# Thirty-six unread bf16 products behind the pairs of heads of an SSD stage: left out

## The chip, the cores and the metric

The kernel runs on one core of one Trainium2 chip. The metric is the device time of one execution in microseconds (us); the time of the kernel before is the median of its runs. Five engines work beside each other and each takes its own instructions in order: TensorE (PE in the profile, its weight loads PEld) for matrix products, VectorE (DVE), ScalarE (ACT), GpSimd (POOL), and SyncE (SP), which here issues DMA transfers. They wait for each other by semaphores.

## The reference, cut to what matters

Two transformer blocks on 512 latent tokens of width 1024. The first block mixes tokens with two groups of heads: a Mamba-2 (SSD) scan of 16 heads and a gated delta rule (GDN) scan of 8 heads, both forwards and backwards over 256 context and 512 latent tokens; its gated and normalised result goes through an output projection and an MLP. The second block has attention and two smaller mixers. For this change only the SSD scan's output on the latent tokens matters, in chunks of 128 tokens:

```python
seg = acum[:, :, :, None, :] - acum[:, :, None, :, :]
lmat = jnp.exp(jnp.where(causal[:, :, None], seg, -jnp.inf))
scores = jnp.einsum('bcihn,bcjhn->bcijh', C_c, B_c) * lmat
y = (jnp.einsum('bcijh,bcjhp->bcihp', scores, xdt)
     + jnp.einsum('bcihn,bchpn->bcihp', C_c, h_prev) * jnp.exp(acum)[..., None])
```

Per head and chunk: a matrix of decays, times the scores, times the inputs; and the carried state, read by decayed queries.

## The kernel before, in words

The program is one launch with a block of code for each engine; the order on each engine is the order in which its code is written, and nothing reorders it. A projection stage streams weights for the first 496 us, then comes the SSD stage that the change touches (496 to 588 us), then the GDN scan (to 722 us), and then projections and MLPs for the rest.

In the SSD stage four chunks of latent tokens (`ci`, 0 to 3) run one after the other, and in each eight pairs of heads (`b` on PE, `hp` on ACT and DVE). One pair on PE is, in its order:

- `decays` (L1251, L1252) for the pair two places on, two products of 512 columns that make the exponents of the decay matrices of both heads and directions in one PSUM bank. It waits until ACT has read that bank's previous contents.
- L1280, four products that put the skip term of the pair into the output bank; L1285, four products with the decay matrix `wmat` of this pair, which wait until DVE has finished that matrix; L1292, eight products with the carried states.
- until now, L1300: two products whose result goes into columns 128 to 511 of bank 1 and is never read. Nothing waits for them and they wait for nothing. They stand behind the pairs `b` 0 to 6 of chunks 0 and 1 and behind pairs 0 to 3 of chunk 2: 18 pairs, 36 products.

Before pair 7 of chunks 0 and 1, PE also makes the scores of the next chunk (`chunk_scores`, L1234) and the decays of its queries (`state_decays`, L1243); the second half of these follows in pair 0 of the chunk.

ACT takes the exponential of each pair's decays (L1944, into two alternating buffers `lbuf`). DVE adds the two directions (L2598) and multiplies by the scores (L2601), which makes `wmat`. Between two pairs DVE also does other work in its own order: the decayed queries (`cpm`, L2583) at the turn of a chunk, the gating of a finished half chunk (`yfm`, L2570), and, from pair 2 of chunk 0 to pair 1 of chunk 2, two elimination steps a pair of a triangular inverse that the GDN stage needs (L2476, L2480), which end with a copy (L2485, `XT`).

That inverse is stored to memory by SP in four transfers (L828 to L832). At pair 4 of chunk 2 PE runs `corner5` (L1167) for the GDN stage; ACT takes its result over (L1896, `PM`) once `corner5` is done and those four stores have landed. ACT's next work for the SSD pairs stands behind that.

Of the kernel before, what the change touches and what calls it, by code (L numbers as in the profile page):

```python
# [18 lines left out]
P = 128  # L19
# [225 lines left out]
def build_kernel(nc, a, out):  # L245
    ctx = ExitStack()
    with ctx:
# [14 lines left out]
        bank = [ctx.enter_context(nc.psum_tensor(f"bank{i}", [P, 512], F32)) for i in range(8)]  # L262
# [15 lines left out]
        def const(n):  # L278
            i = CF.index(n)
            return cf[:, i * P:(i + 1) * P]  # L280

        def cbf(i, n=1):
            return cb[:, i * P:(i + n) * P]
# [158 lines left out]
        def state_at(slot):  # L442

            return v3(hole[slot // 4], KB)[:, 2 * (slot % 4):2 * (slot % 4) + 2, 0:CTX]
# [209 lines left out]
        def ffn_jobs(l):  # L654
            return [(JOB[f"gu{l}{j}"], JOB[f"dn{l}{j}"]) for j in range(3)]

        width = [kc for _, kc, n, _ in JOBS for _ in range(n)]

        def next_width(u):
# [278 lines left out]
        def _(pe):  # L938
# [72 lines left out]
            def gate_transposes(xs, bk):  # L1011

                for n, x in enumerate(xs):
                    mm = pe.transpose(bk[:, n * P:(n + 1) * P], gparts[:, x * P:(x + 1) * P].bitcast(F32), const("ident"))
                mm.then_inc(gates_full, 1)
# [191 lines left out]
            def first_inverse(ci, b):  # L1207

                if (ci, b) == (2, 4):
                    pe.wait_ge(sc_copied, 3)  # L1210
                    pe.wait_ge(row_parts, 11)
                part = {(2, 4): corner5, (2, 6): block5, (3, 3): corner6, (3, 5): block6_t}.get((ci, b))
                if part is corner6:
                    pe.wait_ge(sc_copied, 4)
                if part is not None:
                    for p in range(2):
                        part(0, p)
# [6 lines left out]
            def chunk_scores(ci):  # L1224

                c = NCTX + ci
                if ci:
                    pe.wait_ge(sc_copied, ci)
                if ci == 2:
                    pe.wait_ge(row_parts, 11)  # L1230
                if ci == 3:
                    pe.wait_ge(dt64_ready, 4)
                for gr in range(2):
                    mm = pe.matmul(bank[gr][:, 0:P], bf[64 * gr:64 * gr + 64, c * P:(c + 1) * P],  # L1234
                                   cfm[64 * gr:64 * gr + 64, ci * P:(ci + 1) * P], start=True, stop=True)
                mm.then_inc(sc_full, 1)

            def state_decays(ci, q):

                for d in range(2):  # L1240
                    need(cp_ready, 1, lag=2)
                    i = ci % 2 * 4 + 2 * d + q
                    pe.matmul(bank[2 + d][:, :], halfsel[i // 4][:, i % 4 * P:(i % 4 + 1) * P], grow[4 + ci // 2][:, :], start=True, stop=True  # L1243
                              ).then_inc(cp_full, 1)

            def decays(n):

                ci, hp = n // KB, n % KB
                need(l_ready, 1, lag=2)
                bk = bank[4 + hp % 2]  # L1250
                pe.matmul(bk[:, :], cbf(0), b4(cbf(1, 2), 2), start=True, stop=False)  # L1251
                pe.matmul(bk[:, :], rowcol(ci % 2 * 8 + hp), grow[2 + ci // 2][:, :], start=False, stop=True).then_inc(l_full, 1)  # L1252

            for ci in range(4):
                c = NCTX + ci
                if ci == 0:
                    pe.wait_ge(eps_lo_ready, 1)
                    decays(0)
                    decays(1)
                    chunk_scores(0)  # L1260
                    pe.wait_ge(row_parts, 9)
                    state_decays(0, 0)
                if ci == 3:
                    chunk_scores(3)
                    state_decays(3, 0)

                for b in range(KB):
                    if b == 7 and ci < 2:
                        chunk_scores(ci + 1)
                        state_decays(ci + 1, 0)  # L1270
                    if KB * ci + b + 2 < 4 * KB:
                        decays(KB * ci + b + 2)
                    gr = b // 4
                    if ci and b % 4 == 0:
                        pe.wait_ge(y_taken, 2 * ci - 1 + gr)
                    heads = [(2 * b + e, bank[6 + gr][64 * e:64 * e + 64, (b % 4) * P:(b % 4 + 1) * P]) for e in range(2)]
                    if b % 4 == 0:
                        pe.wait_ge(xd_ready, 2 * ci + gr + 1)
                    for h, dst in heads:
                        pe.matmul(dst, xd[gr][:, h % 8 * 64:(h % 8 + 1) * 64], const("ident"), start=True, stop=False)  # L1280
                    if b == 0:
                        state_decays(ci, 1)
                    need(w_ready)
                    for h, dst in heads:
                        wm = pe.matmul(dst, xtm[:, c * D + h * 64:c * D + (h + 1) * 64], wmat[h % 8 // 4][:, h % 4 * P:(h % 4 + 1) * P], start=False, stop=False)  # L1285
                    wm.then_inc(w_used, 1)
                    if b in (0, 2):
                        pe.wait_ge(cp_ready, 4 * ci + b + 2)
                    for d in range(2):
                        slot = ci if d == 0 else 3 - ci  # L1290
                        for h, dst in heads:
                            mm = pe.matmul(dst, state_at(d * 4 + slot)[64 * gr:64 * gr + 64, h % 8 // 4, h % 4 * 64:(h % 4 + 1) * 64],  # L1292
                                           cpm[d][h % 8 // 4][64 * gr:64 * gr + 64, h % 4 * P:(h % 4 + 1) * P],
                                           start=False, stop=(d == 1))
                    if b % 4 == 3:
                        mm.then_inc(y_full, 1)
                    first_inverse(ci, b)
                    if (ci, b) < (2, 4) and b < 7:
                        for _ in range(2):
                            pe.matmul(bank[1][:, P:4 * P], cbf(0), cbf(0, 3), start=True, stop=True)  # L1300
                    if (ci, b) == (1, 1):
                        gate_transposes((6, 0), bank[0][:, P:3 * P])

# [210 lines left out]
            for l in range(2):  # L1514
# [43 lines left out]
                for b in range(2):  # L1558
                    for e in range(2):
                        for c in range(4):  # L1560
# [3 lines left out]
                                           start=True, stop=True)  # L1564
# [1516 lines left out]
```

## Time and profile before

| | us |
|---|---|
| median of 3 runs | 2356.0 (2354.25 to 2356.33) |
| profiled execution, its own time | 2358.29 |
| its span, first to last instruction | 2356.5 |
| PE busy in the span | 2274.5 (97%) |
| DVE busy in the span | 1322.6 (56%) |
| ACT busy in the span | 951.6 (40%) |
| mean granted TensorE clock | 0.988 of full speed |

PE is busy nearly throughout because most of the program is weight streaming. The shares are means over stages with different limits, so the SSD stage has to be read by itself, from 499 to 557 us of the span. Two levels of the TensorE clock occur in the records: 1.00 (2.4 GHz) and 0.50 (1.2 GHz).

### The profile page before, as it was taken

What the parts mean: (1) busy time and instruction counts of PE and PEld (TensorE: products, weight loads), DVE (VectorE), ACT (ScalarE), POOL (GpSimd) and SP (SyncE); (2) the same over time, 40 slices, a digit from 0 to 9 for tenths busy, and PEclk for the clock granted to TensorE, in tenths of its full rate; (3) what the DMA queues carried; (4) which work ended last, traced back from release to release, by engine and by line L of the source; (5) the groups of instructions that cost most, each with busy time, mean ns of one, the idle gap of its engine ahead of it and who ended that gap; (6) DMA issues with size and microseconds to landing.
All of it is one profiled execution on the core that took longest, in us unless ns stands there. A gap on an engine that the chain in (4) does not pass through costs nothing.

```text
span 2356.5 us, 31246 instructions
## 1 busy us (share of the span) xinstructions
PE 2274.5 (97%) x12510; PEld 1826.9 (78%) x12510; DVE 1322.6 (56%) x2068; ACT 951.6 (40%) x1625; POOL 166.5 (7%) x150
## 2 busy tenths in 40 slices
PE   5999999988999999999999999999999999999998
PEld 4888886755887878888877578888888658888886
DVE  7677777786677355443456644444454654434445
ACT  3555555456326242332445533222244554222222
POOL 0000000000100100000223020000011302000001
PEclk8999999999999999999999999999999999999999
DMA  6343425532544222223222022223323102222222
GB/s 268 108 134 134 175 85 191 176 110 78 157 139 177 98 86 95 99 98 98 98 97 63 28 72 98 92 97 99 98 93 101 56 19 90 99 99 93 95 98 90
DMA packets 117249, 252.29 MB, mean 107 GB/s; under 512 B 45104, under 2 KB 49968, under 8 KB 116208
## 3 DMA queue, kind: packets, MB, share of 16 engines
q1 hardware_dynamic: 102816, 215.15, 27.6%
q0 software_dynamic: 5136, 18.88, 2.4%
q10 hardware_dynamic: 9152, 16.26, 2.0%
q8 instruction: 100, 1.64, 0.3%
q14 instruction: 45, 0.37, 0.0%
HBM read 225.07 MB, written 25.17 MB: 106 GB/s over the span
## 4 chain that ended last, share of the span: by engine, by line
PE 87%; DVE 6%; ACT 3%; DMA 2%; issue 1%; SPq 1%; POOL 0%; ACTq 0%; DVEq 0%; POOLq 0%
PE bank L1426 20%; PE bank L1428 20%; PE bank L1427 20%; PE bank L1040 8%; PE bank L1039 3%; PE bank L1614 2%; PE bank L1307 2%; PE bank L1627 1%; PE bank L1137 1%; PE bank L1139 1%; PE bank L1138 1%; DMA xt<-in_xt 1%; PE bank L1344 1%; DVE smal L2919 1%; PE bank L1658 1%
## 5 line engine op out<-in xcount | busy, mean ns | idle before, releaser
L1979 ACT ACTIVATE whi<-raw 128x1024 fp32r<-128x1024 f32 (+1 forms) x268 | 278.9, 1041 | 899.5 <-PE bank L1428 898.5
L1426 PE MATMUL bank<-ahi,whi 128*128 128x512 f32 x1152 | 452.8, 393 | 4.8 <-DVE alo L2785 3.8
L1428 PE MATMUL bank<-ahi,wlo 128*128 128x512 f32 x1152 | 449.1, 390 | 0.0
L1427 PE MATMUL bank<-alo,whi 128*128 128x512 f32 x1152 | 449.1, 390 | 0.0
L2671 DVE TENSOR_TENSOR wlo<-raw,whi 128x1024 fp32r<-128x1024 f32 (+1 forms) x268 | 324.0, 1209 | 134.8 <-ACT whi L1979 134.6
L1426 PE MATMUL bank<-bhi,whi 128*128 128x512 f32 x736 | 286.6, 389 | 0.0
L1427 PE MATMUL bank<-blo,whi 128*128 128x512 f32 x736 | 286.4, 389 | 0.0
L1428 PE MATMUL bank<-bhi,wlo 128*128 128x512 f32 x736 | 286.4, 389 | 0.0
L1426 PEld LDWEIGHTS bank<-ahi,whi 128*128 128x128 f32 x1152 | 216.7, 188 | 53.8 <-issue 6.6
L1427 PEld LDWEIGHTS bank<-alo,whi 128*128 128x128 f32 x1152 | 216.9, 188 | 45.8 <-issue 1.4
L1428 PEld LDWEIGHTS bank<-ahi,wlo 128*128 128x128 f32 x1152 | 216.7, 188 | 45.3
L3022 POOL TENSOR_TENSOR accx<-accx,sqr 128x512 f32<-128x512 f32 x40 | 69.2, 1730 | 1358.5 <-ACT sqr L2040 1167.0
L1426 PEld LDWEIGHTS bank<-bhi,whi 128*128 128x128 f32 x736 | 138.2, 188 | 28.8 <-issue 0.3
L1428 PEld LDWEIGHTS bank<-bhi,wlo 128*128 128x128 f32 x736 | 138.2, 188 | 28.7
L1427 PEld LDWEIGHTS bank<-blo,whi 128*128 128x128 f32 x736 | 138.2, 188 | 28.6
L2743 DVE TENSOR_TENSOR xr<-bank,xr 128x512 f32<-128x512 f32 x64 | 44.2, 691 | 156.9 <-PE bank L1428 156.9
L1040 PE MATMUL bank<-hhi,whi 128*128 128x512 f32 x272 | 108.2, 398 | 0.0
L1040 PE MATMUL bank<-hhi,wlo 128*128 128x512 f32 x272 | 108.0, 397 | 0.0
L1040 PE MATMUL bank<-hlo,whi 128*128 128x512 f32 x272 | 107.5, 395 | 0.0
L2349 DVE SCALAR_TENSOR_TENSOR cacc<-cbuf,vec,cacc 128x784 f32<-128x784 f32 (+1 forms) x102 | 98.3, 963 | 12.8 <-ACT cacc L1780 10.1
L418 ACT ACTIVATE whi<-raw 128x1024 fp32r<-128x1024 f32 x50 | 53.1, 1064 | 124.7 <-PE bank L1040 119.1
L425 DVE TENSOR_TENSOR wlo<-raw,whi 128x1024 fp32r<-128x1024 f32 x50 | 61.1, 1223 | 68.6 <-ACT whi L418 68.4
(437 smaller groups left out, 3616.2 us busy)
## 6 DMA issues: line engine op xcount, KB each, us to landing
raw<-in_s_gu SPq DMA_DIRECT2D x88, 512.0 KB, 3.3
raw<-in_s_qkvx SPq DMA_DIRECT2D x34, 512.0 KB, 3.6
late_modw<-in_w_mod POOLq DMA_DIRECT2D x32, 512.0 KB, 3.7
raw<-in_s_up SPq DMA_DIRECT2D x32, 512.0 KB, 3.3
raw<-in_s_down SPq DMA_DIRECT2D x32, 512.0 KB, 3.3
raw<-in_s_dn SPq DMA_DIRECT2D x32, 512.0 KB, 3.2
raw<-in_s_win SPq DMA_DIRECT2D x24, 512.0 KB, 3.3
raw<-in_s_zg SPq DMA_DIRECT2D x16, 512.0 KB, 3.8
```

The costliest lines, as they stand in the source:

```text
L418: act.activation(whi[k][:, 0:kc * P], raw[k][:, 0:kc * P], ACT.Identity).then_inc(hi_ready, 1)
L425: dve.tensor_tensor(wlo[k][:, 0:kc * P], raw[k][:, 0:kc * P], whi[k][:, 0:kc * P].bitcast(F32), ALU.subtract).then_inc(lo_ready, 1)
L1039: pe.matmul(cx, w, x[:, s, 0:CTX], start=first, stop=last)
L1040: mm = pe.matmul(lat, w, x[:, s, CTX:TOK], start=first, stop=last)
L1307: mm = pe.matmul(dst[:, o], w[:, o], x[:, o], start=True, stop=True)
L1426: pe.matmul(out, w_hi, x_hi, start=start, stop=False)
L1427: pe.matmul(out, w_hi, x_lo, start=False, stop=False)
L1428: return pe.matmul(out, w_lo, x_hi, start=False, stop=stop)
L1979: act.activation(whi[u % 2][:, 0:width[u + 2] * P], raw[u % 2][:, 0:width[u + 2] * P], ACT.Identity).then_inc(hi_ready, 1)
L2349: after(dve.scalar_tensor_tensor(out=acc, in0=x, scalar=w, in1=acc, op0=ALU.mult, op1=ALU.add))
L2671: dve.tensor_tensor(wlo[u % 2][:, 0:width[u + 2] * P], raw[u % 2][:, 0:width[u + 2] * P], whi[u % 2][:, 0:width[u + 2] * P].bitcast(F32), ...
L3022: pool.tensor_tensor(acc[:, :], acc[:, :], sqr[n % 2][:, :], ALU.add).then_inc(sq_added, 1)
```

## The change

The 36 products of L1300 are left out, with the weight load that belongs to each. Everything else stays as it is, in the same order, on every engine; no wait is added or removed, since these products had none.

```diff
                     if b % 4 == 3:
                         mm.then_inc(y_full, 1)
                     first_inverse(ci, b)
-                    if (ci, b) < (2, 4) and b < 7:
-                        for _ in range(2):
-                            pe.matmul(bank[1][:, P:4 * P], cbf(0), cbf(0, 3), start=True, stop=True)
                     if (ci, b) == (1, 1):
                         gate_transposes((6, 0), bank[0][:, P:3 * P])
```

## Rows read from the trace of the kernel before

**Rows 1.** Busy time by stretch: us, PE, PEld, DVE, ACT, POOL, clock, DMA share, GB/s.

```profile
499.78:551.65 51.87, 46.21 (x393) 25.60 (x394) 48.74 (x123) 36.04 (x134) 3.83 (x8) 0.97 0.13 28
```

**Rows 2.** What DVE waited for between 499.7 and 551 us: total, times, longest.

```profile
DVE cpm L2583 <- PE bank L1243: 3.9, 2, 3.6
```

**Rows 3.** What PE waited for between 507.7 and 551.65 us.

```profile
PE bank L1285 <- DVE wmat L2601: 5.3, 7, 1.4
```

**Rows 4.** Removed line, ns min/median/max; DVE's L2601, 499.7 to 556 us: us, mean ns | idle.

```profile
L1300 PE MATMUL bank<-cb x36: 326/336/527, 502.9 to 554.1; 128*128 128x384 bf16 x36
...
L2601 DVE TENSOR_TENSOR wmat<-wmat,stb 128x256 f32<-128x256 f32 x22 | 9.3, 425 | 0.7
```

**Rows 5.** PE in order of time: start, us, line, [idle before]; turn of chunk 1, then chunk 2.

```profile
539.41 0.44 PE L1285 MATMUL bank<-wmat,xtm 128*64 128x128 f32 x4 [0.60 <-DVE wmat L2601]
...
540.36 0.50 PE L1300 MATMUL bank<-cb 128*128 128x384 bf16 x2
540.79 0.49 PE L1234 MATMUL bank<-cfm,bf 64*128 64x128 f32 x4
...
550.91 0.44 PE L1285 MATMUL bank<-wmat,xtm 128*64 128x128 f32 x4 [0.53 <-DVE wmat L2601]
...
552.20 0.38 PE L1251 MATMUL bank<-cb 128*128 128x512 bf16 x1
...
553.92 0.50 PE L1300 MATMUL bank<-cb 128*128 128x384 bf16 x2
554.25 0.38 PE L1251 MATMUL bank<-cb 128*128 128x512 bf16 x1
...
555.97 0.78 PE L1167 MATMUL bank<-DB,C 32*32 32x32 f32 x64
```

**Rows 6.** DVE in order of time, at the turns into chunk 1 and chunk 2.

```profile
518.10 0.42 DVE L2601 TENSOR_TENSOR wmat<-wmat,stb 128x256 f32<-128x256 f32 x1
518.66 1.29 DVE L2583 TENSOR_TENSOR cpm<-bank,cfm 128x512 f32<-128x512 f32 x2
...
541.82 1.29 DVE L2583 TENSOR_TENSOR cpm<-bank,cfm 128x512 f32<-128x512 f32 x2 [0.34 <-PE bank L1243]
```

**Rows 7.** The chain that ended last, 489 to 592 us: start, us, what.

```profile
540.43 0.43 PE bank L1300 x2
```

**Rows 8.** SP's last store of the inverse, its time to landing, and ACT's work behind it.

```profile
552.64 1.31 SPq L832 DMA_DIRECT2D xv_scratch<-XT  x1
...
xv_scratch<-XT SPq DMA_DIRECT2D x1, 256.0 KB, 4.1
...
556.78 2.06 ACT L1896 ACTIVATE PM<-bank 128x512 f32<-128x512 f32 x4 [2.79 <-PE bank L1167]
```

**Rows 9.** PE waits ahead of pairs, and stretches (columns as rows 1) around a low clock.

```profile
509.55 0.44 PE L1285 MATMUL bank<-wmat,xtm 128*64 128x128 f32 x4 [1.26 <-DVE wmat L2601]
526.10 0.44 PE L1285 MATMUL bank<-wmat,xtm 128*64 128x128 f32 x4 [1.40 <-DVE wmat L2601]
...
527.00:530.00 3.00, 3.00 (x18) 1.78 (x14) 2.86 (x8) 1.89 (x8) 1.64 (x4) 0.50 0.13 39
...
531.00:532.00 1.00, 1.00 (x10) 0.56 (x9) 0.94 (x3) 1.00 (x6) 0.00 (x0) 1.00 0.21 60
```

**Rows 10.** PE at the low clock, in order of time: scores in chunk 0, a pair in chunk 2.

```profile
498.15 0.80 PE L1234 MATMUL bank<-cfm,bf 64*128 64x128 f32 x4
...
561.81 0.61 PE L1251 MATMUL bank<-cb 128*128 128x512 bf16 x1 [3.33 <-ACT lbuf L1944]
...
563.25 0.64 PE L1285 MATMUL bank<-wmat,xtm 128*64 128x128 f32 x4
563.83 1.12 PE L1292 MATMUL bank<-cpm,hst 64*64 64x128 f32 x8
564.88 1.08 PE L1167 MATMUL bank<-PM,DU 32*32 32x32 f32 x64
...
499.78 1.29 DVE L2583 TENSOR_TENSOR cpm<-bank,cfm 128x512 f32<-128x512 f32 x2 [3.60 <-PE bank L1243]
```

## The prediction

> **What bounds the kernel now.** I read the stretch first and the whole second. The page says PE 97% busy, which invites the thought that any product taken from PE is time gained. The table by stretches speaks against it for the place of the change: from 499.78 to 551.65 us, which holds 16 of the 18 places, DVE is busy 48.74 of 51.87 us [rows 1]. It runs 123 instructions there, so most of the missing 3.13 us are the short steps between one instruction and the next (3.13 / 123 = 0.025 us each). The table of waits confirms it: apart from the start of the stage (3.6 us, before any of the removed products), DVE waited for another engine once, 3.9 - 3.6 = 0.3 us, for PE's L1243 [rows 2]. PE in its turn stood still seven times, 5.3 us in total, until DVE had finished a matrix `wmat` [rows 3]. So DVE sets the pace, and PE has room in it. The chain that ended last runs mostly through DVE's lines here and names the removed products four times, 0.43 us each: behind pair 6 of chunk 0, pair 6 of chunk 1 (the row shown), and pairs 2 and 3 of chunk 2 [rows 7]. These four places are the only ones that can give anything, and at each one has to ask what is late next.
>
> **What the removed products take from PE.** In the dense place one pair of them holds PE for 554.25 - 553.92 = 0.33 us; at the turn of a chunk 540.79 - 540.36 = 0.43 us, since the next product is one that starts later [rows 5]. That is 18 x 0.33 = 5.9 us to 18 x 0.43 = 7.7 us of PE's time (a product's own row says 336 ns in the median, but two overlap [rows 4]). The weight loads overlap products and cost nothing more.
>
> **Where it is hidden.** At 14 of the 18 places the next thing that PE does after a short while is to wait for `wmat` from DVE, or it is ahead anyway; there the products fill a wait and their removal makes the wait longer. That cover is DVE's own sequence, which does not change by one instruction. Price: nothing.
>
> **The four places of the chain.** (1) Turn into chunk 1: DVE ends L2601 at 518.10 + 0.42 = 518.52 and starts `cpm` at 518.66, 0.14 later, where the usual step is 0.025 [rows 1, 6]. PE's L1243 was late by 0.11; 0.43 is taken out ahead of it, 0.11 can be gained. (2) Turn into chunk 2: DVE idles 0.34 before `cpm` at 541.82 [rows 6], of which 0.025 is the usual step; PE's products at 540.36 to 540.79 stand on the way from `wmat` to L1243 [rows 5], so 0.31 is gained of 0.43. After that DVE is bound by itself again. (3) and (4), pairs 2 and 3 of chunk 2: here DVE has no more elimination steps and PE is dense, so `corner5`, now at 555.97 [rows 5], comes 2 x 0.33 = 0.66 us sooner, besides what (1) and (2) bring. But ACT's `PM`, the next link, starts at 556.78 and waits also for the last store of the inverse: issued at 552.64, landing 4.1 us later, at 556.74 [rows 8]. The profile puts the wait down to PE because `corner5` ends at 555.97 + 0.78 = 556.75, a hundredth later. Both come at the same time, so taking 0.66 from one gains nothing: the store is late next. The stores hang on DVE's copy and gating, so they move by what (1) and (2) give. From `PM` on everything is shifted by the same amount.
>
> **The sum**: -0.11 - 0.31 = -0.4 us. Against the profiled execution's own time, 2358.29 (span 2356.5 and 1.8 around it), that is 2357.9. That execution lies 2.3 us above the median of the runs shown, so against the median the forecast is 2356.0 - 0.4 = **2355.6 us**.
>
> **What it does to the clock.** This is the one unknown cost. The records show the clock of PE at 0.50 from 527.0 us on, behind a wait of 1.40 us for `wmat`, and at 1.00 again by 531, after PE had been busy without a pause (3.00 of 3.00 us) [rows 9]. A wait of 1.26 us, at 509.55, was not followed by a fall. So with the products in place PE is close to where the clock falls; without them these waits grow by up to three times 0.33 us (the products of pairs 0 to 2 stand ahead of 509.55), and falls will be more frequent. What does one cost? During the one at 527 to 530 us DVE was busy 2.86 of 3.00 us [rows 9]: it lost nothing, since PE's delay fitted into its room. A pair takes 564.88 - 561.81 = 3.07 us at the low clock [rows 10], against 553.92 - 552.20 = 1.72 at the full one, the removed ones not counted [rows 5]; DVE made 22 matrices between 499.7 and 556 us, one in 56.3 / 22 = 2.56 us [rows 4]. PE at the low clock is therefore busy without a pause, and in rows 9 that is what came before the return. So a fall does not last. It costs only where PE's latency is in the open: at the turns and in the dense pairs of chunk 2.
>
> The Trainium skill ("TensorE: Matmul & The Clock Gate", Part 1, The HAM clock gate) speaks against this change: the array's default is the throttled clock, and activity is what releases it, so that taking idle products away from a half idle PE lowers its clock. This trace agrees that the clock falls to 0.50 behind a short wait [rows 9]; by the rule alone the change would lose time, by the rows it loses only where no room is left. The rival below stands on the rows.
>
> **Rivals.**
> *Low clock where it shows (slower).* If PE's clock is low at a turn, the way from `wmat` to `cpm` takes 564.88 - 563.25 = 1.63 us for L1285 and L1292 and 499.78 - 498.15 = 1.63 us for scores and L1243 [rows 10], 3.26 in place of 541.82 - 539.41 = 2.41 now [rows 5, 6]: +0.85 us at each of two turns. In chunk 2, if the clock is low from 550.91 on [rows 5] through pairs 2, 3 and 4, `corner5` ends at 550.91 + 1.63 + 2 x 3.07 + 1.08 = 559.8 [rows 10] in place of 556.75: +3.0. All three together: 2 x 0.85 + 3.0 = +4.7, 2360.7 us; one of them: 2356.9 to 2359. It decides itself by the length of PE's waits ahead of the turns and ahead of 550.9. For it: these waits get longer. Against it: each must hit its place, and the low clock ends after a busy stretch.
>
> *PE is the bound after all (faster).* If DVE's close spacing hid a wait for PE in each pair, all 18 places would come through: -5.9 to -7.7 us, 2348.3 to 2350.1. Against it: DVE's one wait of 0.3 us and PE's 5.3 us of waits [rows 2, 3].
>
> *The chain taken at its word.* Four times 0.43 = -1.7 us, 2354.3. It would need the store not to be late next [rows 8].
>
> **How the numbers follow.** Differences under 0.2% (4.7 us) can hardly be told from no change by a measurement of this kernel. Forecast (-0.4, with the clock low in a place or two that costs under 1 us): 0.66. Chain at its word: 0.10. Low clock where it shows, one or more places: 0.20, of which about half near its full price or, with a further hit such as the second `cpm` of a chunk, above it. PE the bound: 0.04. So faster by over 0.2%: 0.03; within 0.2%: 0.87; slower: 0.10. The range runs from the chain's -1.7 less the 1.7 us by which the lowest of the runs lies under the median (2354.25), about 2352.6, to the slower rival's full price, 2360.7.
>
> **What would show it.** In the profile after: DVE busy about 48.7 us again in a stretch as long, less 0.4; PE busy some 6 us less there; the wait of `cpm` at the turn into chunk 2 under 0.1 us, PE's waits for `wmat` up from 5.3 us to 9 or more; ACT's `PM` starting with the landing of the store and no longer with PE, 0.4 us earlier. Stretches at 0.50 more frequent than the one at 527 us, with DVE busy through them. Wrong it would be if DVE showed new waits for L1243 or for ACT's `lbuf` (the clock, then), or if `PM` began well before 556, or if DVE's instructions themselves stood closer.

## The result, and the profile after

Without the 36 products the kernel takes 2367.73 us (median of 6 executions, 2364.18 to 2372.61), the kernel before 2355.53 us beside it (6 executions): a ratio of 1.0051, 95% interval 1.0038 to 1.0064. It is 12 us slower, where 0.4 us less was forecast, and it lies above the forecast's range, which ended at 2360.7.

The profiled execution took 2368.87 us, its span 2367.1. What answers to [rows 1] and [rows 9] is the table by stretches of the profile after: stretch, us, busy PE, PEld, DVE, ACT, POOL (instructions), granted clock, DMA share, GB/s. First the place of the change as a whole, then, from 506.8 us on, its stretches of one clock and the one behind it.

```profile
499.70:552.00 52.30, 47.95 (x312) 26.63 (x310) 41.59 (x108) 31.78 (x119) 1.92 (x4) 0.67 0.08 18
...
506.80:520.40 13.60, 13.60 (x78) 7.61 (x76) 10.08 (x27) 7.84 (x29) 0.00 (x0) 0.50 0.06 10
520.40:527.30 6.90, 5.06 (x47) 2.74 (x48) 5.97 (x15) 4.08 (x17) 0.00 (x0) 0.99 0.00 0
527.30:547.70 20.40, 20.40 (x114) 11.66 (x116) 16.27 (x43) 12.30 (x45) 1.92 (x4) 0.50 0.09 27
547.70:564.80 17.10, 12.68 (x180) 7.22 (x176) 9.10 (x23) 9.55 (x32) 1.92 (x4) 1.00 0.34 101
564.80:592.10 27.30, 24.12 (x212) 14.78 (x212) 12.49 (x31) 12.91 (x49) 0.00 (x0) 0.50 0.20 52
```

The reader is to see two things. TensorE's clock is at 0.50 (1.2 GHz) for 13.6, 20.4 and 27.3 us, where the kernel before had one stretch of 3.4 us in the place of the change (527.0 to 530.4) and one of 6.8 us behind it (561.2 to 568.0). And PE is busy in the first two of these without any pause, 13.60 of 13.60 and 20.40 of 20.40 us, while DVE, which had 48.74 of 51.87 us [rows 1], has idle time: 41.59 of 52.30.

PE at the falls and at the low clock, in order of time (start, us, line); line numbers above 1295 are three lower than in the kernel before:

```profile
506.09 0.44 PE L1285 MATMUL bank<-wmat,xtm 128*64 128x128 f32 x4 [1.99 <-DVE wmat L2598]
...
514.82 0.64 PE L1285 MATMUL bank<-wmat,xtm 128*64 128x128 f32 x4
...
526.26 0.44 PE L1285 MATMUL bank<-wmat,xtm 128*64 128x128 f32 x4 [1.84 <-DVE wmat L2598]
...
537.17 0.61 PE L1251 MATMUL bank<-cb 128*128 128x512 bf16 x1
...
540.24 0.61 PE L1251 MATMUL bank<-cb 128*128 128x512 bf16 x1
```

A pair takes 540.24 - 537.17 = 3.07 us, the duration of [rows 10], and PE goes on like this over the rest of the chunk. The first fall came behind the wait of 1.99 us ahead of pair 3 of chunk 0, which was 1.26 us before [rows 9], the second behind the wait of 1.84 us ahead of pair 1 of chunk 1, which was 1.40. Where DVE pays for it is seen in its own order of time, the rows that answer to [rows 6]; the first is the start of the stage, the second the `wmat` of pair 6 of chunk 0:

```profile
496.31 1.29 DVE L2580 TENSOR_TENSOR cpm<-bank,cfm 128x512 f32<-128x512 f32 x2 [3.48 <-PE bank L1243]
...
512.33 0.43 DVE L2598 TENSOR_TENSOR wmat<-wmat,stb 128x256 f32<-128x256 f32 x1
...
518.07 1.29 DVE L2580 TENSOR_TENSOR cpm<-bank,cfm 128x512 f32<-128x512 f32 x2 [2.98 <-PE bank L1243]
522.43 1.29 DVE L2580 TENSOR_TENSOR cpm<-bank,cfm 128x512 f32<-128x512 f32 x2 [0.66 <-PE bank L1243]
544.93 1.29 DVE L2580 TENSOR_TENSOR cpm<-bank,cfm 128x512 f32<-128x512 f32 x2 [3.27 <-PE bank L1243]
549.51 1.29 DVE L2580 TENSOR_TENSOR cpm<-bank,cfm 128x512 f32<-128x512 f32 x2 [1.34 <-PE bank L1243]
```

At the two turns DVE waits 2.98 + 0.66 + 3.27 + 1.34 = 8.25 us for PE, against one wait of 0.34 before. That is the loss in chunks 0 and 1: from the first `cpm` to the last of these five it is 549.51 - 496.31 = 53.20 us, and it was 545.02 - 499.78 = 45.24 us (the row of before that starts at 545.02 is in the next fence, with two more of before). The difference is 8.0 us.

```profile
545.02 1.29 DVE L2583 TENSOR_TENSOR cpm<-bank,cfm 128x512 f32<-128x512 f32 x2
...
562.00:567.00 5.00, 5.00 (x86) 2.97 (x87) 2.80 (x9) 2.33 (x9) 0.00 (x0) 0.50 0.24 37
...
587.99 1.55 PE L1381 MATMUL bank<-xtm,cf 128*128 128x512 f32 x3
```

The second row lies in the low stretch of 6.8 us. The third is the end of the SSD stage before; after, it comes at 599.78 (L1378). The stage from its first `cpm` takes 599.78 - 496.31 = 103.47 in place of 587.99 - 499.78 = 88.21 us, 15.3 more: 8.0 to the last `cpm` above, 1.1 up to pair 6 of chunk 2 (PE's L1251 at 567.36, 561.81 before), and 6.2 behind it, in the stretch of 27.3 us. The spans differ by 10.6 only, because the profiled execution of before was 3.5 us later at the start of the stage and met one more low stretch behind it (602.1 to 605.5).

Behind chunk 2 the next link is what the prediction named. ACT and PE in order of time:

```profile
562.34 2.06 ACT L1893 ACTIVATE PM<-bank 128x512 f32<-128x512 f32 x4 [4.17 <-DMA xv_scratch<-XT]
...
567.36 0.61 PE L1251 MATMUL bank<-cb 128*128 128x512 bf16 x1 [5.04 <-ACT lbuf L1941]
```

`PM` now waits for the landing of the store (issued at 557.03, landing 5.2 us later), no longer for `corner5`; PE, which is back at the full clock and through its pairs early, stands still 5.04 us, where it was 3.33 [rows 10], and the clock falls for the third time.

### The profile page after: what moved, and what is told of

Same layout as the page of the kernel before. It is cut to its first block, busy times and chain, and to the rows that moved or that the text cites. A ratio compares the mean times of both kernels' runs of the same rounds, so it can differ in the third digit from the quotient of the medians.

```text
span 2367.1 us, 31174 instructions
## 1 busy us (share of the span) xinstructions
PE 2285.6 (97%) x12474; PEld 1832.3 (77%) x12474; DVE 1324.5 (56%) x2068; ACT 952.1 (40%) x1625; POOL 166.2 (7%) x150
## 4 chain that ended last, share of the span: by engine, by line
PE 90%; DVE 4%; ACT 3%; DMA 2%; issue 1%; SPq 0%; POOL 0%; DVEq 0%; ACTq 0%; POOLq 0%
PE bank L1423 20%; PE bank L1424 20%; PE bank L1425 20%; PE bank L1040 8%; PE bank L1039 3%; PE bank L1611 2%; PE bank L1304 2%; PE bank L1624 1%; PE bank L1137 1%; PE bank L1139 1%; PE bank L1138 1%; DMA xt<-in_xt 1%; PE bank L1341 1%; PE bank L1292 1%; DVE smal L2916 1%
```

## The experiments

The theory formed from this profile: the low clock is the whole loss; PE's own pairs do not end it, and the unread products did. Rivals: the loss belongs to PE's order or time and not to the clock; a fall is short and something else costs. Each ratio is against runs of the kernel before on the same chip. Only unread products differ between the kernels here.

**One chunk at a time.** The condition of the loop gets `and ci != 0`, `and ci != 1` or `and ci != 2`.

```diff
-                    if (ci, b) < (2, 4) and b < 7:
+                    if (ci, b) < (2, 4) and b < 7 and ci != 1:
```

> The products are left out behind the seven pairs of chunk 0 alone. Theory (each chunk's products keep TensorE's clock at 1.00 over their own pairs; pairs alone don't bring it back): the clock falls to 0.50 in chunk 0 behind the wait ahead of pair 3 and comes back at the turn into chunk 1; DVE's instructions lose there about what they lost between the start of the stage and that turn in the profile without any of the products, 3.48 + 0.14 = 3.6 us, and nothing behind it: 2355.5 + 3.6 = 2359 us. Rival (the loss belongs to the later chunks, or only to all three at once): 2355 to 2356 us.

> Left out behind the seven pairs of chunk 1 alone. Theory: the clock falls behind the wait ahead of pair 1 of chunk 1 and stays at 0.50 to the turn into chunk 2, some 20 us; DVE loses 4.49 - 0.14 = 4.4 us: 2360 us, chunk 0 and the stage behind as before. Rival (a fall of the clock does not last, as forecast): 2355 to 2357 us with stretches at 0.50 no longer than the one of before.

> Left out behind pairs 0 to 3 of chunk 2 alone. In the profile without any of the products 10.67 - 4.49 = 6.2 us were lost from chunk 2 on, in a stretch at 0.50 (564.8 to 592.1) that lies behind the last of the products. Theory: these four bring little, since between them PE is dense, and the long stretch came from PE's longer wait for the store of the inverse, which was late because chunks 0 and 1 were slow: 2355.5 +- 1 us. Rival (these four keep the clock up for the rest of chunks 2 and 3): 2355.5 + 6.2 = 2362 us.

Measured: without chunk 0's 1.0021 (1.0012 to 1.0030), +5 us; without chunk 1's 1.0049 (1.0033 to 1.0066), +12 us; without chunk 2's 1.0006 (0.9997 to 1.0015). Leaving out chunk 1's alone costs as much as leaving out all three, more than the 4.4 us expected. The reason stands in its table by stretches and in DVE's order of time:

```profile
522.50:556.60 34.10, 34.06 (x188) 19.27 (x188) 24.72 (x64) 19.40 (x69) 3.84 (x8) 0.50 0.13 40
566.80:590.70 23.90, 23.28 (x211) 14.35 (x210) 12.09 (x31) 9.88 (x37) 0.00 (x0) 0.50 0.20 54
...
541.68 1.29 DVE L2583 TENSOR_TENSOR cpm<-bank,cfm 128x512 f32<-128x512 f32 x2 [3.74 <-PE bank L1243]
547.40 1.29 DVE L2583 TENSOR_TENSOR cpm<-bank,cfm 128x512 f32<-128x512 f32 x2 [2.48 <-PE bank L1243]
```

The stretch at 0.50 that began in chunk 1 ran 34.1 us, through the turn and into chunk 2, where the products were in place (pairs of them start at 549.32 and 553.03), with PE busy 34.06 of it, and the stretch behind was long again. So a low stretch is not ended by the turn for certain, and not by two products a pair for certain either. The fall in chunk 0 did not come in the profile without chunk 0's products (the fastest of its ten executions, 2356.03; the slowest 2364.08): the clock was at 1.00 from 499.7 to 557.8 us, though PE waited 1.97 us ahead of pair 3. The table by stretches, and what DVE waited for between 498 and 552 us:

```profile
499.70:557.80 58.10, 48.65 (x496) 26.80 (x494) 49.06 (x124) 38.31 (x140) 3.83 (x8) 1.00 0.18 46
...
DVE cpm L2583 <- PE bank L1243: 0.8, 2, 0.5
```

Here seven pairs stand without products, in PE's order of the kernel after, and with the clock up DVE waits for L1243 0.8 us in total over both chunks where it was 8.25: that speaks against the first rival. Whether a fall comes seems to differ between executions of one kernel. Of the six executions without any product the two at 2372 us show the lowest granted clock in the mean of the whole span (0.976 and 0.977), the two at 2364 the highest (0.980). What decides in which execution the fall comes was not tried.

**PE occupied, with a quarter of the array.**

```diff
-                            pe.matmul(bank[1][:, P:4 * P], cbf(0), cbf(0, 3), start=True, stop=True)
+                            pe.matmul(bank[1][0:64, P:4 * P], cb[0:64, 0:64], cb[0:64, 0:3 * P], start=True, stop=True)
```

> All 36 products stay, in place, with the same 384 columns in bf16, but each of 64x64 in place of 128x128 (64 rows and 64 columns of the array). Their result is unread as before. Theory (it is not that PE is occupied, but what the products do in the array): the clock falls as without them, 2368 us, or up to 18 x 0.66 = 12 us more, since each pair of products takes 0.66 us at the low clock. Rival (PE occupied is enough): as before, 2355.5 us, with the clock at 1.00 through chunks 0 and 1 but for short falls.

Measured 1.0008 (0.9997 to 1.0019): the rival was right. One fall in chunks 0 and 1, and it lasted 3.4 us, with the pairs and the small products together:

```profile
507.80:511.20 3.40, 3.40 (x25) 2.04 (x26) 3.16 (x11) 2.50 (x11) 0.00 (x0) 0.50 0.14 23
511.20:559.00 47.80, 38.58 (x418) 21.62 (x416) 37.86 (x95) 33.56 (x121) 3.84 (x8) 1.00 0.17 50
```

How much of the array a product fills, all of it or a quarter, was not what mattered here.

**Half and twice the products.** `range(1)` and `range(4)` in place of `range(2)`.

> One product in place of two behind each of the 18 pairs. Theory (what the products add to PE's own pairs keeps the clock up, and it needs a certain amount): with half of it PE's waits are 0.17 us a pair longer than before and falls come more often, and a low stretch lasts longer; some of the loss shows: 2357 to 2364 us. Rival (one is as good as two, since they only have to break up the pairs): 2355 us, low stretches of 3.4 us in chunks 0 and 1.

> Four products in place of two behind each of the 18 pairs. This asks for PE's room by itself, with the clock up. If DVE sets the pace, as the prediction had it, the 18 x 0.33 = 5.9 us more of PE's time show only at the four places of the chain: 0.43 at each turn and 0.33 at each of two dense pairs, the latter up to the landing of the store: +0.9 to +1.5, 2356.4 to 2357 us; the low stretch in chunk 1 may be gone. If PE is the bound: +5.9 to +7.7, 2361 to 2363 us.

One product: 1.0039 (1.0022 to 1.0056), +9 us, at 2364.83 a little above the theory's 2364. Chunk 0 stayed at 1.00 in the profile, chunk 1 did not, with products among its pairs all the time:

```profile
500.00:523.90 23.90, 19.67 (x179) 10.88 (x178) 22.51 (x58) 16.02 (x61) 0.00 (x0) 1.00 0.11 17
523.90:547.80 23.90, 23.85 (x132) 13.75 (x134) 17.36 (x45) 13.41 (x48) 1.92 (x4) 0.50 0.08 23
```

Four products: 1.0018 (1.0004 to 1.0031), +4 us where 0.9 to 1.5 was expected. In the profile the clock was at 1.00 from 498.7 to 560.2 us, and the turns cost what was expected of them:

```profile
516.38 1.29 DVE L2583 TENSOR_TENSOR cpm<-bank,cfm 128x512 f32<-128x512 f32 x2 [0.86 <-PE bank L1243]
539.88 1.29 DVE L2583 TENSOR_TENSOR cpm<-bank,cfm 128x512 f32<-128x512 f32 x2 [0.66 <-PE bank L1243]
```

0.86 and 0.66 in place of 0.14 and 0.34, so 1.0 us more for 5.9 us more of PE's time. The rest of the 4 us, whose interval begins at 0.9, is not accounted for. Part of it may be the clock: four of the ten executions, at 2362 to 2366 us, show a mean granted clock of 0.984 or 0.985, the other six, at 2355 to 2359 us, 0.988 to 0.990.

**Products behind the touched pairs.** Ten unread products ahead of the decays of five later pairs, with all of the 36 and with none of them.

```diff
                 need(l_ready, 1, lag=2)
                 bk = bank[4 + hp % 2]
+                if 23 <= n < 28:
+                    for _ in range(2):
+                        pe.matmul(bk[:, P:4 * P], cbf(0), cbf(0, 3), start=True, stop=True)
```

> All 36 products stay, and ten more go into five pairs behind them: ahead of the decays of pairs 7 of chunk 2 to 3 of chunk 3, into the same PSUM bank, which the decays then overwrite. Theory (products among the pairs bring the clock back): the low stretch behind chunk 2 (6.8 us in the profile before, 10 to 14 in the first experiments) gets shorter by one or two of its steps of 3.4 us, which gives back 1 to 3 us against 5 x 0.33 = 1.7 us of PE's time where PE is dense: 2353 to 2356 us. Rival (PE's time counts there and the clock does not move): 2355 + 1.7 = 2357 us.

> None of the 36 products, but the same ten late ones as in the run with all of them. Theory: the low stretch of 27.3 us behind chunk 2 is shortened to at most 10 us and with it goes the part of the loss that lies behind the touched pairs (from pair 6 of chunk 2 on some 5 us), while chunks 0 and 1 stay slow: 2367.7 - 5 + 1.7 = 2363 to 2365 us. Rival (the loss behind chunk 2 is no matter of the clock there): 2368 to 2370 us.

With all 36: 1.0011 (1.0000 to 1.0022), 2358.18 us, which misses the theory's 2353 to 2356 and is 1.2 us above the rival's 2357. In the profiled execution, the fastest of the ten, the low stretch behind was 6.8 us, as in the profile before, so there was nothing to gain. With none: 1.0032 (1.0021 to 1.0043), +7.5 us in place of +12. Its profile, by stretches and on PE (pair 6 of chunk 2, and the end of the stage):

```profile
506.50:550.90 44.40, 43.66 (x242) 24.70 (x244) 33.36 (x87) 24.99 (x91) 1.91 (x4) 0.50 0.06 16
567.90:578.20 10.30, 7.49 (x98) 4.46 (x100) 4.56 (x14) 5.45 (x21) 0.00 (x0) 0.50 0.21 31
...
570.71 0.82 PE L1253 MATMUL bank<-cb 128*128 128x384 bf16 x2 [4.87 <-ACT lbuf L1944]
...
597.59 3.70 PE L1381 MATMUL bank<-xtm,cf 128*128 128x512 f32 x8
```

With ten products where the long stretch of 27.3 us was, it lasted 10.3, and 4.5 us came back; chunks 0 and 1, without any, ran 44.4 us at 0.50. From pair 6 of chunk 2 to the end of the stage it took 597.59 - 570.71 = 26.9 us, against 599.78 - 567.36 = 32.4 without any product and 587.99 - 561.81 = 26.2 before. So the part of the loss that lies behind the removed products is a matter of the clock too.

**Chunk 1 alone, and two places alone.** The condition `ci == 1` added; and eight products each behind pair 2 of chunk 0 and pair 0 of chunk 1:

```diff
-                    if (ci, b) < (2, 4) and b < 7:
-                        for _ in range(2):
+                    if (ci, b) in ((0, 2), (1, 0)):
+                        for _ in range(8):
```

> Only the 14 products behind the seven pairs of chunk 1 stay; chunks 0 and 2 have none. Theory (the loss is the low clock that PE's own pairs do not end, and chunk 1 is where it lasts): the sum of leaving out chunk 0 alone (+5) and chunk 2 alone (+1), so 2361 us; a fall in chunk 0 is ended by the turn and the products of chunk 1, and chunk 1 is at 1.00. Rival (any low stretch goes on through the later chunks): 2366 us or more.

> 16 products at two places only, eight behind pair 2 of chunk 0 and eight behind pair 0 of chunk 1, where PE's longest waits for DVE lie (1.99 and 1.84 us in the profile without products); the other 16 places have none. Theory in its strong form (it is the falls that have to be prevented; pairs that run at 1.00 stay there): both long stretches at 0.50 are gone and the time is 2355 to 2358 us. Weak form (products are needed among the pairs): falls elsewhere in chunk 1, from where the clock does not come back before the turn: 2361 to 2367 us.

Chunk 1 alone: 1.0021 (1.0009 to 1.0033), 2361.22 us, as expected from the sum. Its profile is of the slowest of the ten executions, 2369.02:

```profile
510.60:524.20 13.60, 13.60 (x78) 7.71 (x76) 10.16 (x28) 7.78 (x29) 0.00 (x0) 0.50 0.06 10
531.10:534.50 3.40, 3.40 (x20) 2.27 (x20) 3.23 (x9) 2.29 (x9) 1.92 (x4) 0.50 0.19 58
534.50:555.00 20.50, 17.86 (x160) 9.59 (x156) 19.20 (x51) 14.88 (x55) 1.58 (x4) 1.00 0.06 17
568.60:592.50 23.90, 23.28 (x207) 14.14 (x207) 12.19 (x31) 9.78 (x36) 0.00 (x0) 0.50 0.20 53
```

The fall in chunk 0, without products, lasted 13.6 us; the one in chunk 1, with them, 3.4 us, and the rest of chunk 1 is at 1.00, as the theory had it. The theory did not have what followed in this execution: the clock fell again at 554.8 in chunk 2, until 565, and then for 23.9 us behind it.

Two places: 0.9997 (0.9985 to 1.0010), 2355.51 us, no difference to the kernel before with 16 products in place of 36, and 14 of the 16 pairs of chunks 0 and 1 without any. The table by stretches, PE's waits ahead of pair 3 of chunk 0 and of pairs 1 and 2 of chunk 1, and DVE at the start and at the turn into chunk 2:

```profile
496.00:557.40 61.40, 49.29 (x498) 27.08 (x496) 50.91 (x128) 40.88 (x150) 3.84 (x8) 1.00 0.20 52
557.40:571.10 13.70, 11.27 (x114) 6.65 (x114) 7.39 (x20) 6.08 (x24) 0.00 (x0) 0.50 0.14 22
...
505.92 0.44 PE L1285 MATMUL bank<-wmat,xtm 128*64 128x128 f32 x4 [0.68 <-DVE wmat L2601]
522.27 0.44 PE L1285 MATMUL bank<-wmat,xtm 128*64 128x128 f32 x4 [0.44 <-DVE wmat L2601]
525.38 0.44 PE L1285 MATMUL bank<-wmat,xtm 128*64 128x128 f32 x4 [0.89 <-DVE wmat L2601]
...
496.14 1.29 DVE L2583 TENSOR_TENSOR cpm<-bank,cfm 128x512 f32<-128x512 f32 x2 [3.60 <-PE bank L1243]
...
540.78 1.29 DVE L2583 TENSOR_TENSOR cpm<-bank,cfm 128x512 f32<-128x512 f32 x2
```

The waits that stood ahead of the falls are cut from 1.99 and 1.84 us to 0.68 and 0.44, no wait in chunks 0 and 1 is over 1.0 us, no fall comes, and the pairs without products stay at 1.00 for 61.4 us. The pairs are the same as in the kernel after; beside the two clusters of products only the clock differs. The strong form of the theory holds in this profile: it is the fall that has to be prevented. It is not prevented for certain: three of the ten executions took 2359 to 2362 us, two of them at a mean granted clock of 0.983 and 0.985, where the seven others have 0.987 to 0.992. Whether it is the shorter wait or the products' own work that keeps the clock up was not tried apart; in every kernel here the two go together.

Over all thirteen profiles of this case, the kernels before and after included: in eight the clock was at 0.50 for 7 to 17 us between 501 and 616 us of the span, and these executions took 2353.6 to 2358.3 us; in five it was so for 51 to 61 us, and these took 2366.1 to 2369.2 us.

**Both together** (two places, and the ten late products), in search of a version that beats both kernels:

> The 16 products at two places (eight behind pair 2 of chunk 0, eight behind pair 0 of chunk 1) and the ten late ones (two each ahead of the decays of pairs 7 of chunk 2 to 3 of chunk 3). Theory: chunks 0 and 1 at 1.00 as with the two places alone; the low stretch behind chunk 2 (13.7 us in that profile) at most 7 to 10 us, which gives back 1 to 2 us after the price of the late products: 2353.5 to 2355.5 us against 2355 to 2356 of the kernel before. Rival (the late products cost what they give back): as before, 2355 to 2357 us.

Measured 1.0014 (1.0004 to 1.0024), 2356.28 us: the rival's value, though in the profile the low stretch behind chunk 2 was 10.2 us in place of 13.7. No version here beats the kernel before by what can be measured.

## Why the prediction was wrong

*What bounds the place* held. DVE sets the pace as long as the clock is up. In the kernel with two places DVE waited for nothing in chunks 0 and 1 and came from the first `cpm` to the last in 540.78 - 496.14 = 44.64 us against 45.24: 0.60 us less, with no product at the turns, where the steps (1) and (2) of the sum had 0.42.

*The store is late next* held: in the profile after, `PM` waits 4.17 us for it, and in the kernel with two places, where the clock was up, 4.75 us.

*What the products take from PE* held in kind: with four products a pair, 5.9 us more of PE's time cost 1.0 us at the turns.

*What it does to the clock* is the step that failed, at one sentence: "So a fall does not last." It was drawn from rows 9, where PE was busy 3.00 of 3.00 us at the low clock and came back. In the profile after, PE was busy without a pause at the low clock for 13.60 and 20.40 us, and with chunk 1's products alone left out for 34.06 of 34.10. Being busy was no sign of the return. Part of what PE was busy with in rows 9 was a pair of the unread products themselves (it starts at 527.05; the next, at 530.85, is behind the return), which the change takes away: the row showed the return with the removed part in it, and was used for the kernel without it. Whether that pair brought the clock back there is not shown, since falls with products among the pairs lasted 23.9 us as well (one a pair).

The numbers for a fall that lasts stood in the prediction: 3.07 us a pair at the low clock against 2.56 us a matrix of DVE. They were used to show that PE would be busy, and not to price what DVE then loses. That price is the term that was put at nothing; it measured 8.0 us in chunks 0 and 1 and 6.2 us behind them. The sign that the prediction gave for being wrong by the clock, new waits of DVE for L1243, is what came. Of its other signs, PE's waits for `wmat` did not grow to 9 us: with the low clock they are three, 4.1 us in total, between 497 and 552 us.

*The slower rival* had the right mechanism and places, and prices too small. It counted one chain of latency at the low clock at each turn, +0.85 us. With a fall that lasts, PE loses 3.07 - 2.56 = 0.5 us to DVE in the mean of the pairs and arrives at the turn with the sum of it. It took up pair 3 of chunk 0 as soon as `wmat` was there; the `wmat` of pair 6 is ready at 512.33 + 0.43 = 512.76, and PE comes to it at 514.82, 2.06 us late. With the 0.85 that makes 2.91, and DVE's wait at that turn is 2.98; at the next it is 3.27, and at the second `cpm` of each chunk 0.66 and 1.34 again. That is 8.25 us at the turns in place of 1.7. The third place, chunk 2 up to `corner5`, was priced at 3.0 for a low clock from 550.91 on; in this profile it was not hit, since the clock was at 1.00 from 547.70 to 564.80. In its place came a stretch behind all removed products, 27.3 us at 0.50, which cost 6.2 us and stood nowhere in the prediction. The rival's chance, 0.20, was too low because falls were taken to be short, and its full price of 4.7 us because PE was taken to come to each turn without a lag and nothing was priced behind the removed products.

The Trainium skill's sentence that was weighed ("TensorE: Matmul & The Clock Gate", Part 1, The HAM clock gate: the throttled clock is the default, and activity releases it) was nearer to the outcome than the rows as they were read. These profiles bear it out only in part: the kernel lost clock when the products were taken away, but PE recorded as busy for 20.40 of 20.40 us had not got it back.

## What to carry to other kernels

A product that nobody reads can pay for itself: before it is taken out, look at the granted clock in its stretch, and price a kernel without it also at the low clock through the whole loop, not only for as long as the low stretches with it in place last. Work that is hidden under another engine's pace at full clock may not be at half clock: compare the period of the loop at both levels with the pace (here 1.72 and 3.07 against 2.56 us), and multiply the difference by the number of steps until the next point where the other engine waits. If products are added to hold a clock, places ahead of the longest waits are worth trying before one behind every step: 16 at two places did here what 36 did at eighteen.

## What the runs showed of the hardware that was not expected

PE recorded as busy without a pause did not bring the clock back: with the pairs and the work of the turn alone, which are mostly products of 128 columns on half or a quarter of the array, it stayed at 0.50 for 13.6 and 20.4 us. Falls among pairs with two unread bf16 products of 384 columns lasted 3.4 us in three profiles (the kernel before, the one with the small products, and chunk 1 alone), on a quarter of the array as well as on all of it. Nor do such products always end a low stretch: in the kernel with one behind each pair it ran 23.9 us, and a stretch of 34.1 us ran on over two pairs that had theirs. What ends it stays open.

In chunks 0 and 1 falls came behind single waits of 1.3 to 2.0 us, though not in every profile: a wait of 1.97 us was followed by none in one, one of 1.99 us by a fall in another. In the kernel with chunk 1's products alone the fall at 554.8 us in chunk 2 came behind two waits of 1.06 and 0.87 us.
